# The output projection's weights in four column quarters, and two pieces of TensorE work moved, in a decoder step's attention

## The chip, the cores and the metric

The kernel runs on one core of a Trainium2 chip, in one launch. The metric is the device time of that core in microseconds, the median over several runs. The core's engines are TensorE (PE), VectorE (DVE), ScalarE (ACT) and GpSimd (POOL); SyncE (SP) issues most of the transfers. Each engine works through its own list of instructions in order, and waits on semaphores for the others.

## The reference

One layer of a decoder is computed for 512 prompt tokens and for 8 samples of one token each, with D = 1024 channels, all in f32. Each of its three sub-layers ends in `x <- LayerNorm(ALPHA * x + f(x))`:

1. a mixer (an RG-LRU group and a convolution group, side by side),
2. cross-attention with 4 heads of 256 into 256 memory tokens. Cut to what matters:

```
q = (x @ w_q)                     # 512 prompt tokens and 8 samples
s = q . k * 256**-0.5             # prompt: keys computed from mem_prompt; samples: keys from a cache
p = softmax(s)
o = p . v                         # samples: values from a cache
x = layer_norm(ALPHA * x + o @ w_o, ln2_g, ln2_b)
```

3. a mixture of experts: 64 routed experts, 8 per token, and a shared one.

The samples' cached keys and values are 8 times 256 x 1024 each (1 MB per sample), and `w_o` is 1024 x 1024 (4 MB).

## The kernel before

The engines' programs are written out by hand. Activations lie transposed, channels in 8 chunks of 128 partitions and the 520 tokens along the free dimension; the normalization behind the attention is done for two halves of 260 tokens, so that the first half is projected before the samples' values are summed. PSUM is used as four banks of 128 x 1024 (`bank`). The list `GROUPS` (L57 to L77) fixes which group of products takes which bank, in turn, and which engine empties it: `open_group` (L839) waits until the group four places earlier has been emptied, by ScalarE ("A") or VectorE ("V"). A group's place in this list is thus its place in TensorE's order.

The order of the attention is the list `ATTENTION` (L66), walked by TensorE (L1105) and by ScalarE (L1626): `sc0` to `sc3` are the prompt's scores for 128 tokens each, `pt0` to `pt3` the transposed probabilities, `o0` to `o7` the sums over the values for 128 channels each. Behind them come `xa0` to `xa7`, the output projection of the first half by chunks of 128 output channels (`project`, 8 products over the input channels each). Among these stand `ssT`, which turns the sampled scores, and `spT`, which turns their probabilities. Then follow `mean2a` (the mean over channels), `os` (the samples' sum over the cached values, 64 products for 8 samples) and inside it, ahead of the sixth sample, `var2a` (the variance). `osT` turns the result of `os` into the place of the 8 last tokens, and `xb0` to `xb7` project the second half.

VectorE computes the sampled scores itself (`sample_scores`, L2041): for each sample eight reductions of a product of cached keys and the query, copied to all partitions. At the end of sample b it raises `s_ss` to b + 1. Only then come the residuals of `xa0` and `xa1`, the softmax of the sampled scores (L2124 to L2128), the residuals of the further chunks, and `half_center`, `half_square_sum` and `half_scale` of the normalization. ScalarE squares (`half_squares`, L1646), takes the root of the variance (`half_root`, L1651), copies the four heads of `os` (L1670) and then `osT` (L1675), and applies gain and bias (`half_gain`).

Memory: `arena` has three parts of 8192 columns. During the sampled scores the first holds the queries of the 8 samples (`q_all`), the second the keys of samples 0 to 3 (`cache(1, b)`, 2048 columns each) and the third those of samples 4 to 7. `w_o` takes the whole second part as `wslot(1)`, in which each of the 8 rows of input channels has 1024 columns. The values take the places of the queries (samples 0 to 3) and of the keys in the third part (samples 4 to 7). SyncE (L521 to L532) therefore waits for `s_ss` at 2, loads value 0, waits for 4, loads `w_o` in four issues of 256 output columns each, then value 1, and so on; the five last values wait for all eight samples.

Of the kernel before, what the change touches and what calls it, by code (L numbers as in the profile page):

```python
# [14 lines left out]
P = 128  # L15
D = 1024
KC = D // P
# [32 lines left out]
for _n, _k in PAR_SPEC:  # L50
# [6 lines left out]
GROUPS = [(f"x{t}", "AV"[t % 2]) for t in range(TT)] + [("par", "V")]  # L57
# [6 lines left out]
GROUPS += [(f"q{c}", "A") for c in range(KC)] + [("qs", "A")]  # L64

ATTENTION = ["sc0", "sc1", "sc2", "pt0", "sc3", "pt1", "pt2", "pt3", "o0", "o1", "o2", "o3", "o4", "o5", "o6", "o7",  # L66
             "xa0", "xa1", "ssT", "xa2", "spT", "xa3"]
GROUPS += [(name, "V" if name[0] == "x" else "A") for name in ATTENTION]

GROUPS += [(f"xa{c}", "V") for c in range(4, KC)]  # L70
GROUPS += [("mean2a", "V"), ("var2a", "A"), ("os", "A"), ("osT", "A")]
GROUPS += [(f"xb{c}", "V") for c in range(KC)]
GROUPS += [("h1a0", "A"), ("mean2b", "V"), ("h3a0", "V"), ("var2b", "A"), ("h1b0", "A"), ("rt0", "A"),
           ("rt1", "A"), ("x20", "A"), ("rtT", "A"), ("x21", "A"), ("x22", "A")]
# [76 lines left out]
def decoder_step(nc: bass.Bass, ins, outs):  # L151
# [3 lines left out]
    with ExitStack() as ctx:  # L155
        def sb(name, shape, dt=F32):
            return ctx.enter_context(nc.sbuf_tensor(name, shape, dt))

        def sem(name):
            return ctx.enter_context(nc.semaphore(name))  # L160
# [5 lines left out]
        arena = sb("arena", [P, 3 * 8192])  # L166
# [19 lines left out]
        def rows(at, k):  # L186
            return act_mem[:, at:at + k * T].rearrange("p (k t) -> p k t", k=k)
# [34 lines left out]
        oT = rows(A3, KC)  # L222
# [4 lines left out]
        sp = mk_mem[0:32, 1344:1600]  # L227
# [82 lines left out]
        def value_cache(b):  # L310
            return cache(0, b) if b < 4 else cache(2, b - 4)

        def wslot(n):
            return arena[:, 8192 * n:8192 * n + 8192].rearrange("p (k n) -> p k n", k=KC)

        def cache(n, b):
            return arena[:, 8192 * n + 2048 * b:8192 * n + 2048 * b + 2048].rearrange("p (m n) -> p m n", m=2)

# [23 lines left out]
        s_wo_wd = [sem(f"s_wo_wd{n}") for n in range(4)]  # L342
# [37 lines left out]
        s_ss = sem("s_ss")  # L380
# [50 lines left out]
        def emptied(eng, g):  # L431

            who = GROUPS[g][1]
            n = sum(1 for _, w in GROUPS[:g + 1] if w == who)
            eng.wait_ge(s_emA if who == "A" else s_emV, n)

        def wait_out(eng, name):

            emptied(eng, GID[name])

        def wait_full(eng, name):
            eng.wait_ge(s_full, GID[name] + 1)

        def bank(name):
            return psum[:, PAIR.get(name, (GID[name] + 3) % 4), :]
# [15 lines left out]
        def _(sp):  # L461
# [12 lines left out]
            def big_cache(n, slot, src, b0):  # L474
                for b in range(4):
                    sp.dma_start(cache(slot, b), src[0, b0 + b].rearrange("(p m) h d -> p m (h d)", m=2)).then_inc(
                        s_load[n], 16)
# [38 lines left out]
            def values(b):  # L516
                sp.dma_start(value_cache(b), I["cache_mem_v"][0, b].rearrange("(p m) h d -> p m (h d)", m=2)).then_inc(
                    s_val[b // 2], 16)


            sp.wait_ge(s_ss, 2)  # L521
            values(0)
            sp.wait_ge(s_ss, 4)
            w_o = I["w_o"][0].rearrange("(k p) n -> p k n", p=P)
            for n in range(4):
                sp.dma_start(wslot(1)[:, :, 256 * n:256 * n + 256], w_o[:, :, 256 * n:256 * n + 256]).then_inc(s_wo_wd[n], 16)
            values(1)
            sp.wait_ge(s_ss, 6)
            values(2)
            sp.wait_ge(s_ss, NS)  # L530
# [307 lines left out]
        def _(pe):  # L838
            def open_group(name):  # L839
                g = GID[name]  # L840
                if g >= 4:
                    emptied(pe, g - 4)
                return bank(name)

            def mm(out, lhsT, rhs, first, last):
                return pe.matmul(out, lhsT, rhs, start=first, stop=last)  # L846
# [65 lines left out]
            for j in range(first, 2 * RC):  # L912
                if j == RC:
                    turn_states()
                name = ("zv", "zs")[j // RC] + str(j % RC)
                wide(name, lambda k: wslot(0)[:, k, j * P:(j + 1) * P], lambda k: xT[:, k, :], range(KC))
            pe.wait_ge(s_load[1], 16 * KC)
            for j in range(2 * RC):
                name = ("zu", "zg")[j // RC] + str(j % RC)
                at = (j + RC) % (2 * RC)  # L920
# [167 lines left out]
            def half_wide(name, w, act, ks, h, before=None):  # L1088

                ps = open_group(name)  # L1090
                for n, k in enumerate(ks):
                    if before is not None:
                        before(k)
                    last = mm(ps[:, 0:HALF], w(k), act(k)[:, HALF * h:HALF * h + HALF], n == 0, n == len(ks) - 1)
                last.then_inc(s_full, 1)

            def project(name, h):
                j = int(name[2])
                if h == 0 and j % 2 == 0:
                    pe.wait_ge(s_wo_wd[j // 2], 16)  # L1100
                if (h, j) == (0, 0):
                    wait_out(pe, "o7")
                half_wide(name, lambda k: wslot(1)[:, k, j * P:(j + 1) * P], lambda k: oT[:, k, :], range(KC), h)

            for name in ATTENTION:  # L1105
                if name == "ssT":
# [7 lines left out]
                else:  # L1114
                    {"sc": scores, "pt": turn_probs}[name[0:2]](int(name[2]))

            for c in range(4, KC):
                project(f"xa{c}", 0)

            def half_mean(name, h, turn_no):  # L1120
# [3 lines left out]
            def half_var(name, h):  # L1124
                pe.wait_ge(s_sqsum, h + 1)
                half_wide(name, lambda k: mean_d[:, :], lambda k: xsum[:, 0, :], range(1), h)
# [3 lines left out]
            wait_out(pe, "spT")  # L1130
            ps = open_group("os")
            for b in range(NS):
                if b == 5:
                    half_var("var2a", 0)
                if b % 2 == 0:
                    pe.wait_ge(s_val[b // 2], 16 * 2)
                for m in range(2):
                    for h in range(XH):
                        last = mm(ps[32 * h:32 * h + NS, 0:XD], weigh[:, m, h, b, :],
                                  value_cache(b)[:, m, XD * h:XD * h + XD], (b, m) == (0, 0), (b, m) == (NS - 1, 1))  # L1140
            last.then_inc(s_full, 1)
            wait_out(pe, "os")
            pe.wait_ge(s_os, XH - 1)
            ps = open_group("osT")
# [4 lines left out]
            for c in range(KC):  # L1149
                project(f"xb{c}", 1)  # L1150
# [163 lines left out]
            def down_few(b, part):  # L1314
                _, wd = ew(part)
                for k in range(2):
                    for h in range(2):
                        last = mm(psum[LCAP * h:LCAP * h + LCAP, 0, 0:512], hidT[:, b, LCAP * k:LCAP * k + LCAP],
                                  wd[:, k, 512 * h:512 * h + 512], k == 0, k == 1)
                return last  # L1320
# [11 lines left out]
            def down(b, part, cap=CAP):  # L1332
                _, wd = ew(part)
                for n in range(2):
                    for k in range(2):
                        last = mm(psum[0:cap, 0, 512 * n:512 * n + 512], hidT[:, b, cap * k:cap * k + cap],
                                  wd[:, k, 512 * n:512 * n + 512], k == 0, k == 1)
                return last
# [161 lines left out]
        def _(act):  # L1500
# [22 lines left out]
            for j in range(2 * RC):  # L1523
                c = j % RC
# [118 lines left out]
            def half(ap, h):  # L1643
                return ap[:, HALF * h:HALF * h + HALF]

            def half_squares(h):  # L1646
                for k in range(KC):
                    act.wait_ge(s_sub, norm_at[0] + k + 1)
                    act.activation(half(sq[:, k, :], h), half(xT[:, k, :], h), ACT.Square).then_inc(s_sq, 1)  # L1649

            def half_root(name, h):  # L1651
                wait_full(act, name)
                act.activation(half(rstd[:, :], h), bank(name)[:, 0:HALF], ACT.Sqrt, bias=eps_t[:, 0:1]).then_inc(s_emA, 1)
# [10 lines left out]
                act.activation(half(sh1[:, "ab".index(name[2]), :], h), bank(name)[:, 0:HALF], ACT.Silu).then_inc(s_emA, 1)  # L1664

            half_squares(0)
            half_root("var2a", 0)
            wait_full(act, "os")
            for h in range(XH):
                last = act.activation(o_s[:, XD * h:XD * h + XD], bank("os")[32 * h:32 * h + NS, 0:XD], ACT.Copy)  # L1670
                if h < XH - 1:
                    last.then_inc(s_os, 1)
            last.then_inc(s_emA, 1)
            wait_full(act, "osT")
            act.activation(oT[:, :, SEQ:T], bank("osT")[:, 0:64].rearrange("p (j b) -> p j b", j=KC), ACT.Copy).then_inc(s_emA, 1)  # L1675
            half_gain(0)
# [161 lines left out]
        def _(dve):  # L1838
# [202 lines left out]
            def sample_scores(b):  # L2041
                if b % 4 == 0:
                    dve.wait_ge(s_load[6 + b // 4], 16 * 4)
                if b % 2 == 0:
                    dve.wait_ge(s_qall[b // 2], 16 * 2)
                kc = cache(1 + b // 4, b % 4)
                for m in range(2):
                    for h in range(XH):
                        ins = dve.tensor_tensor_reduce(junk, kc[:, m, XD * h:XD * h + XD], q_all[:, b, XD * h:XD * h + XD],  # L2049
                                                       1.0, 0.0, ALU.mult, ALU.add, ss[:, m, 4 * b + h:4 * b + h + 1])  # L2050
                        if (m, h) != (1, XH - 1):
                            link(ins)
                ins.then_inc(s_ss, 1)
                dve.wait_ge(s_ss, b + 1)
# [443 lines left out]
```

## Time and profile before

| | |
|---|---|
| median of 3 runs | 1148.14 us |
| lowest and highest run | 1147.12 and 1151.25 us |
| span of the profiled execution (the page gives no other time of it) | 1144.5 us |
| PE busy | 1087.3 us, 95% |
| DVE, ACT, POOL busy | 43%, 25%, 21% |
| chain that ended last, by engine | PE 73%, DVE 17%, DMA 5%, ACT 2% |
| mean granted TensorE clock | 0.989 |

A row of a timeline gives the start in the span, the time it took, engine, line, operation, the tiles written and read, their shapes and the number of instructions merged; in square brackets stands how long the engine had been idle just before and who released it. A product of f32 operands appears as two records, so a chunk of 8 products has 16. A granted clock of 1.00 is 2.4 GHz and 0.50 is 1.2 GHz.

### The profile page before, as it was taken

The page shows a single profiled execution, that of the slowest core. Times are in us where ns is not written, and L with a number is a line of the kernel's source. Part 1 is how long each engine was busy: PE and PEld are TensorE (multiplying, and loading weights), DVE is VectorE, ACT ScalarE, POOL GpSimd, SP SyncE. Part 2 cuts the span into 40 slices and gives each one's busy share as a digit, 9 for nine tenths or more (in the row PEclk, how much of TensorE's full clock was granted, in tenths as well). Part 3 has the DMA queues.
Part 4 walks back from the last instruction along what each step waited for, and adds up shares of the span by engine and source line. Part 5 has one row for each costly group of instructions (what it writes and reads, how often), then busy time and mean ns, then how long its engine had stood idle before and what let it go on. Part 6 is the DMA issues. An engine that isn't in the chain of part 4 may idle for free.

```text
span 1144.5 us, 22216 instructions
## 1 busy us (share of the span) xinstructions
PE 1087.3 (95%) x8721; PEld 718.2 (63%) x8721; DVE 495.5 (43%) x1429; ACT 288.6 (25%) x615; POOL 243.9 (21%) x300
## 2 busy tenths in 40 slices
PE   7999998999997989989999999999999999999996
PEld 6888665877883857847555555555556555565531
DVE  0349999224028444681323333233343333423236
ACT  1112163004033041411223222222222322222220
POOL 3120040000000001031333323333333333343300
PEclk9999999999999999998999999999999999999998
DMA  9630315016034853175999999999999999999696
GB/s 331 271 147 1 147 32 183 2 60 251 3 119 148 323 200 133 56 288 217 394 404 409 412 411 415 408 410 414 410 417 410 403 421 407 409 416 387 256 387 262
DMA packets 67122, 319.77 MB, mean 279 GB/s; under 512 B 11069, under 2 KB 17429, under 8 KB 40397
## 3 DMA queue, kind: packets, MB, share of 16 engines
q1 hardware_dynamic: 51269, 278.60, 61.2%
q0 software_dynamic: 14336, 35.48, 8.2%
q10 hardware_dynamic: 1424, 4.35, 1.0%
q8 instruction: 70, 1.15, 0.4%
q14 instruction: 23, 0.19, 0.0%
HBM read 299.36 MB, written 28.58 MB: 287 GB/s over the span
## 4 chain that ended last, share of the span: by engine, by line
PE 73%; DVE 17%; DMA 5%; ACT 2%; issue 2%; SPq 0%; POOL 0%; DVEq 0%; ACTq 0%; POOLq 0%
PE psum L846 65%; PE psum L861 8%; DVE act_mem L1884 7%; DVE mk_mem L2049 2%; DMA arena<-y_rows 2%; DMA mk_mem<-x_rows,idx_x 2%; DMA arena<-in_w_in_dram 2%; DVE act_mem L2105 0%; ACT act_mem L1649 0%; DVE act_mem L2256 0%; DVE act_mem L1984 0%; ACT act_mem L1658 0%; DVE act_mem L2268 0%; DVE act_mem L1982 0%; DVE act_mem L1952 0%
## 5 line engine op out<-in xcount | busy, mean ns | idle before, releaser
L846 PE MATMUL psum<-arena,act_mem 128*32 128x128 f32 (+6 forms) x5488 | 493.4, 365 | 2.1 <-ACT act_mem L1764 1.1
L846 PEld LDWEIGHTS psum<-arena,act_mem 128*32 128x32 f32 (+4 forms) x5488 | 254.4, 120 | 192.6 <-issue 96.7
L846 PE MATMUL psum<-act_mem,arena 128*128 128x260 f32 (+1 forms) x1472 | 328.7, 386 | 8.9 <-DMA arena<-in_w_o_dram 3.8
L846 PEld LDWEIGHTS psum<-act_mem,arena 128*128 128x128 f32 x1472 | 281.0, 196 | 54.1 <-DMA arena<-in_w_o_dram 4.7
L861 PE MATMUL psum<-ident,act_mem 128*128 128x128 f32 (+6 forms) x488 | 79.3, 291 | 15.6 <-DMA act_mem<-in_x_prompt_dram 4.5
L754 POOL DMA_INDIRECT y_rows<-act_mem,idx_y x35 | 39.2, 1120 | 237.4 <-DVE act_mem L2319 214.4
L2317 DVE COPY act_mem<-psum 64x512 f32<-64x512 f32 x35 | 24.3, 693 | 124.7 <-PE psum L846 124.7
L1884 DVE SCALAR_TENSOR_TENSOR act_mem<-act_mem,wcb 128x511 f32<-128x511 f32 (+29 forms) x120 | 77.8, 730 | 0.1
L861 PEld LDWEIGHTS psum<-ident,act_mem 128*128 128x128 f32 (+6 forms) x488 | 57.3, 169 | 29.1 <-issue 17.5
L846 PEld LDWEIGHTS psum<-act_mem 128*96 128x96 bf16 (+5 forms) x419 | 29.9, 123 | 58.2 <-issue 54.6
L2310 DVE SCALAR_TENSOR_TENSOR act_mem<-act_mem,psum 128x128 f32<-128x128 f32 x35 | 12.2, 348 | 114.3 <-ACT act_mem L1720 114.3
L1716 ACT ACTIVATE act_mem<-psum 128x768 f32<-128x768 f32 (+1 forms) x63 | 45.1, 716 | 55.5 <-PE psum L861 55.5
L846 PE MATMUL psum<-act_mem 128*96 128x6 bf16 (+7 forms) x419 | 56.5, 262 | 2.0 <-ACT act_mem L1739 1.3
L1720 ACT ACTIVATE act_mem<-psum 128x192 f32<-128x192 f32 x35 | 11.6, 331 | 162.6 <-PE psum L846 162.6
L861 PE MATMUL psum<-ident,mk_mem 128*128 128x128 f32 (+4 forms) x316 | 43.7, 281 | 7.3 <-issue 4.0
L861 PEld LDWEIGHTS psum<-ident,mk_mem 128*128 128x128 f32 (+4 forms) x316 | 36.9, 183 | 19.2 <-issue 14.8
L747 POOL DMA_INDIRECT y_rows<-act_mem,idx_y x26 | 26.7, 1026 | 93.8 <-ACT act_mem L1755 52.9
L846 PE MATMUL psum<-arena,kv_mem 128*128 128x512 f32 x96 | 41.8, 593 | 1.2 <-ACT kv_mem L1539 1.2
L1745 ACT ACTIVATE act_mem<-psum 64x512 f32<-64x512 f32 x35 | 20.7, 591 | 77.1 <-PE psum L846 77.1
L680 POOL MEMSET act_mem<- 128x512 f32 x1 | 0.5, 525 | 184.2 <-PE psum L861 184.2
L754 POOL DMA_INDIRECT y_rows<-act_mem,more_y x35 | 34.6, 989 | 10.7 <-DVE idx_x L2286 5.8
L1506 ACT ACTIVATE act_mem<-psum,par 128x520 f32<-128x520 f32 x24 | 16.1, 696 | 77.0 <-PE psum L846 76.8
(291 smaller groups left out, 890.8 us busy)
## 6 DMA issues: line engine op xcount, KB each, us to landing
arena<-in_w_e_dram SPq DMA_DIRECT2D x192, 1024.0 KB, 10.2
arena<-y_rows SPq DMA_DIRECT2D x8, 2048.0 KB, 20.4
arena<-in_w_in_dram SPq DMA_DIRECT2D x16, 512.0 KB, 17.7
arena<-in_cache_mem_k_dram SPq DMA_DIRECT2D x8, 1024.0 KB, 8.6
arena<-in_cache_mem_v_dram SPq DMA_DIRECT2D x8, 1024.0 KB, 11.8
arena<-in_w_v_dram SPq DMA_DIRECT2D x1, 4096.0 KB, 24.4
arena<-in_w_k_dram SPq DMA_DIRECT2D x1, 4096.0 KB, 13.9
arena<-in_w_out_dram SPq DMA_DIRECT2D x1, 4096.0 KB, 14.1
```

Source lines behind the costliest of these rows:

```text
L747: gp.indirect_dma_start(out=y_rows[:, :].rearrange("r (h n) -> (r h) n", h=2), out_offset=bass.IndirectOffsetOnAxis(ap=idx_y[:, n:n + 1], ...
L754: gp.indirect_dma_start(out=y_rows[:, :], out_offset=bass.IndirectOffsetOnAxis(ap=idx[0:cap, n:n + 1], axis=0), in_=src[at:at + cap, :], i ...
L846: return pe.matmul(out, lhsT, rhs, start=first, stop=last)
L861: return pe.transpose(out, in_, ident[0:n, 0:n])
L1506: act.activation(out, two(bank(name)), func, **kw).then_inc(s_emA, 1)
L1716: return act.activation(xgT[:, b, :, 0:cap], psum[:, 1, :].rearrange("p (k s) -> p k s", k=KC)[:, :, ROWS_AT:ROWS_AT + cap], ACT.Copy)
L1720: return act.activation(silu[:, b, 0:192], psum[:, 2, 512 * b:512 * b + 192], ACT.Silu)
L1745: act.activation(out[0:LCAP, 0:512], psum[0:LCAP, 0, 0:512], ACT.Copy)
L1884: return dve.scalar_tensor_tensor(out, in0, w, in1, ALU.mult, ALU.add)
L2049: ins = dve.tensor_tensor_reduce(junk, kc[:, m, XD * h:XD * h + XD], q_all[:, b, XD * h:XD * h + XD], 1.0, 0.0, ALU.mult, ALU.add, ss[:, m ...
L2310: dve.scalar_tensor_tensor(silu[:, b, 0:P], silu[:, b, 0:P], gates[:, n, 0:1], psum[:, 2, 512 * b + 192:512 * b + 320], ALU.mult, ALU.mult)
L2317: dve.tensor_copy(out[0:LCAP, 512:1024], psum[LCAP:2 * LCAP, 0, 0:512])
```

## The change

`w_o` still comes in four issues of 256 output columns, but each lies in one piece of 2048 columns, `out_quarter(n)`, which is exactly the place of the keys of sample n. SyncE issues quarter n when `s_ss` has reached n + 1, and values 0 and 1 behind the second and the fourth quarter. `ssT` stands behind `xa3` and `spT` behind `xa4`. On TensorE `var2a` stands behind the whole of `os`; on ScalarE the root of `var2a` stands behind the four copies of `os` and ahead of the copy of `osT`; the group list follows. VectorE's program is not edited.

```
 ATTENTION = [..., "o7",
-             "xa0", "xa1", "ssT", "xa2", "spT", "xa3"]
+             "xa0", "xa1", "xa2", "xa3", "ssT", "xa4", "spT"]
-GROUPS += [(f"xa{c}", "V") for c in range(4, KC)]
-GROUPS += [("mean2a", "V"), ("var2a", "A"), ("os", "A"), ("osT", "A")]
+GROUPS += [(f"xa{c}", "V") for c in range(5, KC)]
+GROUPS += [("mean2a", "V"), ("os", "A"), ("var2a", "A"), ("osT", "A")]
...
+        def out_quarter(n):
+            return arena[:, 8192 + 2048 * n:8192 + 2048 * n + 2048].rearrange("p (k n) -> p k n", k=KC)
...
-            sp.wait_ge(s_ss, 2)
-            values(0)
-            sp.wait_ge(s_ss, 4)
             w_o = I["w_o"][0].rearrange("(k p) n -> p k n", p=P)
             for n in range(4):
-                sp.dma_start(wslot(1)[:, :, 256 * n:256 * n + 256], w_o[:, :, 256 * n:256 * n + 256]).then_inc(s_wo_wd[n], 16)
-            values(1)
+                sp.wait_ge(s_ss, n + 1)
+                sp.dma_start(out_quarter(n), w_o[:, :, 256 * n:256 * n + 256]).then_inc(s_wo_wd[n], 16)
+                if n % 2 == 1:
+                    values(n // 2)
             sp.wait_ge(s_ss, 6)
             values(2)
...
-                half_wide(name, lambda k: wslot(1)[:, k, j * P:(j + 1) * P], lambda k: oT[:, k, :], range(KC), h)
+                at = P * (j % 2)
+                half_wide(name, lambda k: out_quarter(j // 2)[:, k, at:at + P], lambda k: oT[:, k, :], range(KC), h)
...
-            for c in range(4, KC):
+            for c in range(5, KC):
                 project(f"xa{c}", 0)
...
             for b in range(NS):
-                if b == 5:
-                    half_var("var2a", 0)
                 if b % 2 == 0:
                     pe.wait_ge(s_val[b // 2], 16 * 2)
...
             last.then_inc(s_full, 1)
+            half_var("var2a", 0)
             wait_out(pe, "os")
...
             half_squares(0)
-            half_root("var2a", 0)
             wait_full(act, "os")
             for h in range(XH):
                 last = act.activation(o_s[:, XD * h:XD * h + XD], bank("os")[32 * h:32 * h + NS, 0:XD], ACT.Copy)
...
             last.then_inc(s_emA, 1)
+            half_root("var2a", 0)
             wait_full(act, "osT")
```

## Rows read from the trace of the kernel before

**Rows 1.** Waits between 345 and 460 us: who waited, for whom, total, times, longest.
```profile
PE psum L846 <- DMA arena<-in_w_o_dram: 3.8, 1, 3.8
```

**Rows 2.** Timeline of TensorE in the attention stretch.
```profile
351.52 13.97 PE L846 MATMUL psum<-act_mem,kv_mem 128*128 128x512 f32 x32 [1.20 <-ACT act_mem L1620]
369.33 8.97 PE L846 MATMUL psum<-act_mem,arena 128*128 128x260 f32 x32 [3.84 <-DMA arena<-in_w_o_dram]
379.07 0.38 PE L861 MATMUL psum<-ident,mk_mem 128*32 128x128 f32 x2 [0.77 <-DVE mk_mem L2049]
...
383.18 17.80 PE L846 MATMUL psum<-act_mem,arena 128*128 128x260 f32 x80
402.03 0.70 PE L846 MATMUL psum<-act_mem,mean_d 128*128 128x260 f32 x2 [1.05 <-DVE act_mem L2079]
402.67 4.50 PE L846 MATMUL psum<-arena,act_mem 128*8 128x256 f32 x80
...
409.60 2.78 PE L846 MATMUL psum<-arena,act_mem 128*8 128x256 f32 x48
414.07 0.66 PE L861 MATMUL psum<-ident,mk_mem 8*128 8x8 f32 x8 [1.70 <-ACT mk_mem L1670]
415.04 33.51 PE L846 MATMUL psum<-act_mem,arena 128*128 128x260 f32 x144 [0.31 <-ACT act_mem L1675]
```

**Rows 3.** Stretches: length, busy time of each engine, granted clock, DMA share, GB/s.
```profile
351.50:365.50 14.00, 13.97 (x32) 5.99 (x32) 12.96 (x61) 4.18 (x7) 0.00 (x0) 1.00 0.23 79
...
369.30:375.00 5.70, 5.67 (x18) 4.66 (x19) 5.28 (x25) 0.00 (x0) 0.00 (x0) 0.70 1.10 349
393.00:401.00 8.00, 7.98 (x37) 6.58 (x35) 1.71 (x4) 0.00 (x0) 0.00 (x0) 1.00 0.21 89
415.00:420.00 5.00, 4.96 (x15) 4.06 (x16) 0.00 (x0) 4.98 (x9) 1.18 (x5) 0.66 1.11 360
```

**Rows 4.** Timeline of VectorE: sampled scores (first and last of 128 instructions), centring, sum of squares.
```profile
349.08 0.42 DVE L2049 CUSTOM_DVE_ANT_0 mk_mem<-arena 128x256 f32<-128x256 f32 x1
...
378.84 0.08 DVE L2049 DVE_READ_ACCUMULATOR2_ANT mk_mem<- 128x1 f32 x1
...
402.78 2.77 DVE L2089 TENSOR_TENSOR act_mem<-act_mem,psum 128x260 f32<-128x260 f32 x8 [0.80 <-PE psum L846]
...
406.16 2.75 DVE L2105 TENSOR_TENSOR act_mem<-act_mem 128x260 f32<-128x260 f32 x6
```

**Rows 5.** Issues on SyncE's queue: start, time in the queue, line.
```profile
364.00 5.42 SPq L526 DMA_DIRECT2D arena<-in_w_o_dram  x4
369.46 11.71 SPq L517 DMA_DIRECT2D arena<-in_cache_mem_v_dram  x7
```

**Rows 6.** The source view of L526, the four issues of w_o.
```profile
DMA to landing us min/median/max: 5.3/9.5/12.6
```

**Rows 7.** Timeline of ScalarE: three table loads and what stands around them.
```profile
261.47 0.60 ACT L1594 ACTIVATE kv_mem<-psum 128x512 f32<-128x512 f32 x1 [1.20 <-PE psum L846]
262.09 1.28 ACT L1506 ACT_TABLE_LOAD   x1
...
365.53 0.60 ACT L1624 ACTIVATE act_mem<-psum 128x512 f32<-128x512 f32 x1 [1.12 <-PE psum L846]
...
406.08 1.28 ACT L1653 ACT_TABLE_LOAD   x1
409.71 0.48 ACT L1653 ACTIVATE rstd<-psum,eps_t 128x260 f32<-128x260 f32 x1 [2.35 <-PE psum L846]
412.44 1.58 ACT L1670 ACTIVATE mk_mem<-psum 8x256 f32<-8x256 f32 x4 [2.26 <-PE psum L846]
414.76 0.22 ACT L1675 ACTIVATE act_mem<-psum 128x64 f32<-128x64 f32 x1 [0.75 <-PE psum L861]
...
462.82 1.28 ACT L1664 ACT_TABLE_LOAD   x1
464.12 0.39 ACT L1664 ACTIVATE act_mem<-psum 128x260 f32<-128x260 f32 x1
```

## The prediction

> **What bounds the kernel now.** I read the waits of the attention stretch first, then TensorE's timeline there, then the granted clock of the same stretch, and then VectorE, SyncE's queue and ScalarE, each for the thing TensorE waits for. TensorE carries the end: the page has it busy for 95% of the span, and 73% of the chain that ended last is its own. So a microsecond is won only where TensorE stands still or runs slowly, and the change touches two such places. The waits name the first, 3.8 us for a transfer of `w_o` [rows 1]; the second is the cut in `os`, seen in the timeline.
>
> There the first place runs so: the values' product for the prompt (`o0` to `o7`) ends at 351.52 + 13.97 = 365.49, and the projection `xa0` starts at 369.33, after 3.84 us of waiting for `w_o` [rows 2]. Its two chunks `xa0`, `xa1` take 8.97 us, where five chunks (80 records) take 17.80, so 7.1 for two [rows 2]. The clock view says why: 1.00 before, 0.70 on average over 369.3 to 375.0 [rows 3], a stretch at the lower of the two levels (1.2 against 2.4 GHz). Lost there: 0.30 x 5.7 = 1.7 us. Then 0.77 us of waiting for the sampled scores ahead of `ssT` [rows 2]. The second place: `os` runs its first five samples in 4.50 us, `var2a` blocks the queue, the last three samples run at 409.60, then ScalarE's copies, `osT`, a copy, and `xb0` starts at 415.04; the clock is down again there, 0.66 over 415 to 420, so 0.34 x 5 = 1.7 us [rows 2, 3].
>
> **Part 1: `w_o` by quarters.** VectorE's sampled scores run from 349.08 to 378.84 + 0.08 = 378.92, 3.73 us a sample, so samples 0 to 3 end at 352.8, 356.5, 360.3 and 364.0 [rows 4]. Before, all four issues stand behind the fourth of these, at 364.00 [rows 5]. After, quarter n goes when sample n is done. The number and size of the transfers stay: four of 1 MB. Landing took 5.3 to 12.6 us, the upper figure with five other megabytes in the queue [rows 6]. Even by the slowest, the quarters are there at 365.4, 369.1, 372.9 and 376.6, while their first readers start no sooner than 366.2 (`xa0`), 373.2 (`xa2`), 380.6 (`xa4`) and 388 (`xa6`). The wait for `w_o` goes away.
>
> What is late next is ScalarE's copy of `o7`, which frees the operand: 365.53 + 0.60 = 366.13 [rows 7]. So `xa0` starts at about 366.18: gain 369.33 - 366.18 = 3.15 us. A gap of 0.7 us remains there. The clock was 1.00 throughout `o0` to `o7` behind a gap of 1.20 [rows 2, 3], so I take it to stay up: gain 1.7 us, with 0 as the other end.
>
> On SyncE's queue the moved issues pass values(0) and values(1). values(0) now goes behind two quarters and values(1) still behind the fourth; neither is read before `os`, 30 us later. values(3) to (7) keep their release, the last sampled score, and were issued by 369.46 + 11.71 = 381.17 [rows 5]. Their queue is emptier, since three megabytes of `w_o` have left earlier: no loss, and a gain only where somebody waits for them, which nobody does. Do the earlier writes slow VectorE while it reads keys? Samples 0 to 3 took 364.00 - 349.08 = 14.92 us with hardly a transfer running (DMA share 0.23), samples 4 to 7, beside transfers at full rate (1.10), 378.92 - 364.00 = 14.92 as well [rows 3 to 5]: nothing is charged.
>
> **Part 2: `ssT` two chunks later.** `xa0` to `xa3` take at most 4 x 3.56 = 14.2 us from 366.18 and end near 380.4, behind the last sampled score at 378.92. The wait of 0.77 us goes: gain 0.77 (a bank wait cannot replace it: `ssT` takes `xa0`'s bank, which VectorE frees 0.5 us behind its last score). VectorE's order does not change: `xa0`, `xa1`, then the maximum of `ssT`, now at about 380.8 instead of 380.3. The 0.5 us does not reach TensorE, because `xa4` (3.5 us) lies between `ssT` and `spT`, as `xa2` did before. If that cover were gone, it would cost those 0.5 us.
>
> So the projections end at 383.18 + 17.80 = 400.98 before, and 3.15 + 1.70 + 0.77 = 5.62 us sooner after: 395.36. The mean's wait and product keep their length, and `os` starts at 402.67 - 5.62 = 397.05.
>
> **Part 3: `var2a` behind `os`.** `os` took 409.60 + 2.78 - 402.67 = 9.71 us with `var2a` and its wait inside; its two pieces alone are 4.50 + 2.78 = 7.28. Gain 2.43: `os` ends at 404.33. The wait added to PE's queue is for the square sum. VectorE's chain from the mean to that sum took 402.78 to 406.16 + 2.75 = 408.91 [rows 4]; 5.62 sooner that is 403.29, 1.0 us ahead of the end of `os`. So `var2a` does not wait and lies beside ScalarE's copies of `os` (4 in 1.58 us).
>
> What this part costs lies on ScalarE. The copies of `os` now come ahead of the square root, whose function table must be loaded, 1.28 us. A load stands right in front of the instruction that needs it, also behind a waiting copy: at L1594 the copy waits until 261.47, and the load follows it at 262.09 although ScalarE was idle before [rows 7]. So load and root now lie between the copies and the copy of `osT`: 0.02 + 1.28 + 0.02 + 0.48 + 0.02 + 0.22 + 0.06 = 2.10 us from the last copy's end to `xb0`, where it was 415.04 - 414.02 = 1.02. `osT` itself (0.66) is covered by the load. Loss 1.08. The ends: if the load were hidden in the wait ahead of the copies, as it was in the wait ahead of the root until now, nothing of its 1.28 would remain and the loss would be zero (`osT` then ends last); 1.08 is the other end, and I take it.
>
> The Trainium skill, "ScalarE: Activation LUTs", section "What ACT_TABLE_LOAD costs", speaks against the move: it counts about 2.66 us for each switch, a drain of 1.38 beside the load. The trace has a switch with nothing to wait for, and there the next instruction started 464.12 - 462.82 = 1.30 us after the load began, right behind the work ahead of it [rows 7]. By the page the time would be an estimated 1.4 us longer, 1142.5; the trace does not bear it out, and it has its place below as (e).
>
> **Sum.** 5.62 + 2.43 - 1.08 = 6.97 us sooner at the start of `xb0` (408.07 instead of 415.04). The remaining term is the clock at `xb0`. Before, it fell behind a gap of 1.70 and a short burst [rows 2, 3]. After, TensorE runs through `os` and `var2a` without a stop to 405.0, then has gaps of about 1.0 and 1.4 us around `osT`. Behind the 1.05 at `mean2a` it stayed up (the records of `os` take 56 ns each there, 58 in the second piece), behind 1.70 it fell, and the new gaps lie between these or near the lower one; bounds 0 and a gain of 1.7 us. I take 0, since the burst between the gaps is again only `osT`.
>
> Behind `xb0` everything is released in turn: `w1_s` and expert 0 by the end of `os`, expert 1 by `xb7`, the further experts by the routing that follows. All of it shifts with TensorE; `half_scale` on VectorE ends near 412.5, and the first residual `xb0` is full no sooner than 411.6, with three more banks free. So the profiled execution's 1144.5 us becomes 1137.5. The page gives no time of that execution but its span; the median of the runs, 1148.14, is 3.64 above, and I leave that as it is: 1137.5 + 3.6 = 1141.1 us.
>
> **Rivals.** (a) The clock stays up at `xb0` too: another 1.7 us, 1139.4. For it: the gaps are each shorter than the one that preceded the fall. Against: together they are longer. Chance 0.27.
> (b) The gain is partly given back by TensorE's clock, which falls once or twice more in places where the shifted work leaves short bursts, at 1.7 us each: 1142.8 to 1144.5. Chance 0.10. For it: two falls in 50 us already, neither needing more than a few microseconds of gaps.
> (c) The later stages do not follow: the expert loop starts at its old time, and the gain is hidden, 1148. For it: the DMA engines are busy for over 90% of the expert loop. Against: what starts their stream waits for TensorE or for the routing. That the quarters arrive no sooner than before, so that the edit does not do what it says, belongs here too, and the landing times speak against it. Chance 0.06.
> (d) Slower. `var2a`, and with it the normalization, stands behind all eight values, where it needed six before. Place: the last pair inside `os`, needed at about 397.05 + 0.75 x 7.28 = 402.5. Every microsecond that it lands later delays `xb0` by one; it eats the whole gain from 409.5 on, and a landing at 415.5 gives 1154. Against: the DMA engines were at 0.21 over 393 to 401 [rows 3], so the last value was down at about 395, and now it has less ahead of it. Chance 0.03.
> (e) The switch to the root's table costs more than its load, because ScalarE must first finish the copies. The most that the rows allow from a load's start to its root is 409.71 - 406.08 = 3.63 us, which holds a wait for TensorE [rows 7]; that is 2.3 us over the 1.30 taken, 1143.4. Against: the row of 1.30. Chance 0.04. (The table rule of the Trainium skill quoted above is of this kind.)
>
> **How the numbers follow.** The forecast has the remaining 0.50. About 0.5% (5.7 us) is what a measurement of this kernel can tell from no change; the border lies at 1142.4. The forecast lies 1.3 us below it, and the runs shown spread over 4 us, so 0.43 of its 0.50 counts as faster, with 0.26 of (a) and 0.05 of (b) and (e): 0.74. Slower: (d), 0.03. The rest, 0.23, is no change. The range reaches from (a) with 2 us for the runs' spread and a clock fall less later on, 1137.4, to the end of (b), 1144.7.
>
> **What would show it.** In the changed kernel's timeline the gap behind `o7` should be about 0.7 us and released by ScalarE's copy; `xa0` to `xa3` should take 14 us at a clock of 1.00; `ssT` should follow without a wait; `os` should be one piece of 7.3 us; ScalarE should show copies, table load, root, copy in that order; and `xb0` should start near 408. The prediction is wrong if `xa0` still waits for a transfer, if `os` waits for a value, if the load is found ahead of the copies, or if `xb0` starts 7 us sooner and the span does not follow.

## The result and the profile after

The changed kernel took 1141.34 us in the median (1139.96 to 1143.96) beside 1147.63 before (four runs now, where the table ahead of the prediction has three): a ratio of 0.9936, with a 95% interval of 0.9916 to 0.9956, or 7.3 us less. The two medians differ by 6.3 us; here and below, what is called less or more in us is worked out from the ratio and the median before. Measured again beside some of the experiments (`e7_changed_again` below) it was 0.9949 (0.9929 to 0.9969), 5.9 us less. The forecast was 1141.1, 7 us less.

Of TensorE's timeline these rows answer to [rows 2]. Line numbers are 3 higher after the change: L846 is now L849, L861 is L864.

```profile
349.67 1.22 PE L864 MATMUL psum<-ident,act_mem 128*128 128x128 f32 x8 [2.00 <-DVE act_mem L2039]
351.67 1.97 PE L864 MATMUL psum<-ident,act_mem 128*128 128x128 f32 x8 [0.78 <-DVE act_mem L2039]
354.84 16.90 PE L849 MATMUL psum<-act_mem,kv_mem 128*128 128x512 f32 x32 [1.21 <-ACT act_mem L1623]
372.47 14.27 PE L849 MATMUL psum<-act_mem,arena 128*128 128x260 f32 x64 [0.73 <-issue]
386.58 0.38 PE L864 MATMUL psum<-ident,mk_mem 128*32 128x128 f32 x2
...
402.48 0.71 PE L849 MATMUL psum<-act_mem,mean_d 128*128 128x260 f32 x2 [1.05 <-DVE act_mem L2082]
403.11 7.09 PE L849 MATMUL psum<-arena,act_mem 128*8 128x256 f32 x128
410.13 0.70 PE L849 MATMUL psum<-act_mem,mean_d 128*128 128x260 f32 x2
411.90 0.66 PE L864 MATMUL psum<-ident,mk_mem 8*128 8x8 f32 x8 [1.06 <-ACT mk_mem L1672]
413.81 31.83 PE L849 MATMUL psum<-act_mem,arena 128*128 128x260 f32 x144 [1.25 <-ACT act_mem L1678]
```

The reader is to see three things. `xa0` starts 0.73 us behind `o7` instead of 3.84 (the row names no releaser, but ScalarE's copy of `o7` ends at 371.78 + 0.60 = 372.38, just ahead of it), and `xa0` to `xa3` are one piece of 14.27 us. `ssT` follows without any wait. `os` is one piece of 7.09 us. And one thing that was not forecast: `o0` to `o7` took 16.90 us where they had taken 13.97. The stretches (columns as in [rows 3]) say why: the clock was down behind the softmax's gaps here, and up at `xb0`, the reverse of before. A stretch in which the granted clock goes down to the lower of its two levels is called a fall below.

```profile
349.60:354.80 5.20, 3.19 (x16) 2.42 (x16) 4.28 (x21) 3.48 (x7) 0.52 (x1) 0.59 0.00 0
354.80:371.80 17.00, 16.90 (x32) 7.09 (x32) 15.75 (x73) 4.20 (x8) 0.00 (x0) 0.83 0.92 312
372.40:386.60 14.20, 14.13 (x65) 12.20 (x66) 9.60 (x43) 0.00 (x0) 0.00 (x0) 1.00 0.63 236
...
413.80:419.00 5.20, 5.20 (x24) 4.53 (x25) 4.79 (x10) 3.05 (x7) 0.28 (x1) 1.00 1.09 313
```

ScalarE, answering to [rows 7]: copies of `os`, table load, root, copy of `osT`. The root follows its load after 1.29 us.

```profile
410.27 1.57 ACT L1672 ACTIVATE mk_mem<-psum 8x256 f32<-8x256 f32 x4 [3.77 <-PE psum L849]
411.87 1.28 ACT L1656 ACT_TABLE_LOAD   x1
413.16 0.48 ACT L1656 ACTIVATE rstd<-psum,eps_t 128x260 f32<-128x260 f32 x1
413.54 0.22 ACT L1678 ACTIVATE act_mem<-psum 128x64 f32<-128x64 f32 x1
```

SyncE's queue, answering to [rows 5], and the landing of `w_o`, answering to [rows 6]: the quarters go two by two between the values, and the slowest lands in 7.0 us instead of 12.6.

```profile
355.25 4.12 SPq L528 DMA_DIRECT2D arena<-in_w_o_dram  x2
359.41 0.58 SPq L521 DMA_DIRECT2D arena<-in_cache_mem_v_dram  x1
362.72 4.11 SPq L528 DMA_DIRECT2D arena<-in_w_o_dram  x2
366.87 17.03 SPq L521 DMA_DIRECT2D arena<-in_cache_mem_v_dram  x7
...
DMA to landing us min/median/max: 5.1/5.7/7.0
```

The view that says most is one that the prediction does not use: the chain of waits of this stretch alone (345 to 420 us), its shares by line. Before:

```profile
by line: PE psum L846 40.7%; DVE mk_mem L2049 36.1%; issue 5.0%; DVE act_mem L2105 3.5%; ACT act_mem L1649 3.3%; ACT act_mem L1610 2.6%; ACT mk_mem L1670 2.0%; PE psum L861 1.7%; DVE small L2023 1.6%; DVE act_mem L2036 1.2%; DVE act_mem L20
```

and after:

```profile
by line: PE psum L849 82.0%; PE psum L864 3.3%; ACT act_mem L1613 2.6%; issue 2.1%; ACT mk_mem L1672 2.0%; ACT L1656 1.7%; DVE small L2026 1.6%; ACT act_mem L1623 1.4%; DVE act_mem L2039 1.2%; ACT rstd L1656 0.6%; DVE act_mem L2082 0.6%; DV
```

VectorE's sampled scores (L2049) carried 36% of this stretch before, from the softmax up to `ssT`; after the change they are gone from the chain, and TensorE's products carry 82%. The wait for `w_o` was thus not a wait that set the end by itself: it lay beside the scores.

### The profile page after: what moved, and what is told of

The parts are those of the page before. It is cut to its first block, busy times and chain, and to the rows that moved or that the text cites. A ratio compares the mean times of both kernels' runs of the same rounds, so it can differ in the third digit from the quotient of the medians.

```text
span 1142.2 us, 22216 instructions
## 1 busy us (share of the span) xinstructions
PE 1090.5 (95%) x8721; PEld 719.4 (63%) x8721; DVE 495.1 (43%) x1429; ACT 288.6 (25%) x615; POOL 243.5 (21%) x300
## 4 chain that ended last, share of the span: by engine, by line
PE 80%; DVE 14%; DMA 2%; ACT 2%; issue 2%; SPq 0%; POOL 0%; DVEq 0%; ACTq 0%; POOLq 0%
PE psum L849 72%; PE psum L864 8%; DVE act_mem L1887 7%; DMA arena<-in_w_in_dram 2%; DMA mk_mem<-x_rows,idx_x 1%; DVE act_mem L2259 0%; DVE act_mem L1987 0%; ACT act_mem L1661 0%; DVE act_mem L2271 0%; DVE act_mem L2108 0%; DVE act_mem L1985 0%; DVE act_mem L1955 0%; DVE act_mem L1959 0%; DVE act_mem L1956 0%; DVE act_mem L1957 0%
## 5 line engine op out<-in xcount | busy, mean ns | idle before, releaser
L849 PE MATMUL psum<-arena,act_mem 128*32 128x128 f32 (+6 forms) x5488 | 494.6, 366 | 2.1 <-ACT act_mem L1767 1.1
L849 PEld LDWEIGHTS psum<-arena,act_mem 128*32 128x32 f32 (+4 forms) x5488 | 254.7, 121 | 192.9 <-issue 96.7
L849 PE MATMUL psum<-act_mem,arena 128*128 128x260 f32 (+1 forms) x1472 | 326.7, 385 | 7.4 <-DMA arena<-in_w_in_dram 3.2
L849 PEld LDWEIGHTS psum<-act_mem,arena 128*128 128x128 f32 x1472 | 280.1, 195 | 51.6 <-issue 4.0
L864 PE MATMUL psum<-ident,act_mem 128*128 128x128 f32 (+6 forms) x488 | 80.5, 293 | 17.4 <-issue 4.3
L864 PEld LDWEIGHTS psum<-ident,act_mem 128*128 128x128 f32 (+6 forms) x488 | 57.9, 170 | 31.5 <-issue 18.0
L849 PEld LDWEIGHTS psum<-act_mem 128*96 128x96 bf16 (+5 forms) x419 | 29.9, 123 | 59.0 <-issue 55.4
L849 PE MATMUL psum<-act_mem 128*96 128x6 bf16 (+7 forms) x419 | 56.5, 262 | 2.0 <-ACT act_mem L1742 1.3
L864 PE MATMUL psum<-ident,mk_mem 128*128 128x128 f32 (+4 forms) x316 | 43.7, 281 | 4.1 <-issue 3.1
L864 PEld LDWEIGHTS psum<-ident,mk_mem 128*128 128x128 f32 (+4 forms) x316 | 37.0, 183 | 15.6 <-issue 13.4
L849 PE MATMUL psum<-arena,kv_mem 128*128 128x512 f32 x96 | 41.8, 593 | 1.2 <-ACT kv_mem L1542 1.2
```

The source lines that it names most:

```text
L864: return pe.transpose(out, in_, ident[0:n, 0:n])
```

## The experiments

All are compared with the kernel before on the same chip, in 6 to 12 timed runs each. In the traces I use one length that does not depend on when the kernel's start was over: from the last turn of probabilities (`pt3`) to the start of `os`. It was 402.67 - 349.22 = 53.45 us before and 403.11 - 351.67 = 51.44 in the changed kernel's trace above. The two last turns of before, `pt2` and `pt3`:

```profile
347.22 1.09 PE L861 MATMUL psum<-ident,act_mem 128*128 128x128 f32 x8 [2.01 <-DVE act_mem L2036]
349.22 1.09 PE L861 MATMUL psum<-ident,act_mem 128*128 128x128 f32 x8 [0.91 <-DVE act_mem L2036]
```

**The change without its third part** (`e1_no_var_move`): the changed kernel with these lines put back, and on ScalarE the root ahead of the copies again.

```
-GROUPS += [("mean2a", "V"), ("os", "A"), ("var2a", "A"), ("osT", "A")]
+GROUPS += [("mean2a", "V"), ("var2a", "A"), ("os", "A"), ("osT", "A")]
...
+                if b == 5:
+                    half_var("var2a", 0)
```

> The quarters and the later ssT, with var2a inside os and its root ahead of the copies as in the kernel before. Theory (the sum of the prediction): the first two parts bring 3.15 + 1.70 + 0.77 = 5.6 us by themselves, the third 1.35 more; so about 1142.0 us beside 1147.6 before, xa0 starting 0.7 us behind o7, and 9.7 us again for os with var2a inside. Rival: the gain of the change is mostly the clock falling less often by chance; then this kernel stands where the changed one does, 1141.3, or back at 1147.6, without regard to the part left out.

Measured: 0.9971 (0.9954 to 0.9988), 3.3 us less (1.4 to 5.3), short of the 5.6. In its trace `pt3` to `os` took 47.63 us, 5.82 less than before, as the sum had it; here the clock stayed up in the whole stretch. That falls there in the other executions make up the difference fits the two traces of the changed kernel, but is not shown run by run.

```profile
350.56 1.09 PE L864 MATMUL psum<-ident,act_mem 128*128 128x128 f32 x8 [0.90 <-DVE act_mem L2040]
352.86 13.97 PE L849 MATMUL psum<-act_mem,kv_mem 128*128 128x512 f32 x32 [1.21 <-ACT act_mem L1624]
367.56 14.27 PE L849 MATMUL psum<-act_mem,arena 128*128 128x260 f32 x64 [0.73 <-issue]
...
398.19 4.50 PE L849 MATMUL psum<-arena,act_mem 128*8 128x256 f32 x80
...
409.59 0.66 PE L864 MATMUL psum<-ident,mk_mem 8*128 8x8 f32 x8 [1.69 <-ACT mk_mem L1674]
410.56 31.83 PE L849 MATMUL psum<-act_mem,arena 128*128 128x260 f32 x144 [0.31 <-ACT act_mem L1679]
```

The last two rows also show that at `xb0`, behind the very gaps of [rows 2] (1.7 and 0.31), the clock did not fall this time: 31.83 us for the piece that took 33.51 before. The same gaps bring the clock down in one execution and not in another.

**The third part alone** (`e2_var_move_alone`): the kernel before with the last hunks of the diff only.

```
+GROUPS += [("mean2a", "V"), ("os", "A"), ("var2a", "A"), ("osT", "A")]
...
             last.then_inc(s_full, 1)
+            half_var("var2a", 0)
```

> Only the third part on top of the kernel before: os in one piece, var2a behind it, its root behind the copies. Theory: os 2.4 us shorter, 1.1 us given back by the table load and the root ahead of the copy of osT; xb0 1.35 us sooner against the end of xa7, so about 1146.3 us. Rival: the table load is no loss (it was hidden or would be anyway): 1145.2; or the wait for the square sum is only moved: 1147.6.

Measured: 0.9974 (0.9960 to 0.9989), 3.0 us less; the lower end of the interval is 1.3. In the trace `os` starts at 403.79 and `xb0` at 414.48: 10.69 us where it was 12.37, a gain of 1.68, somewhat above the 1.35. What the timing shows beyond that is not explained.

```profile
403.79 7.09 PE L846 MATMUL psum<-arena,act_mem 128*8 128x256 f32 x128
...
414.48 31.83 PE L846 MATMUL psum<-act_mem,arena 128*128 128x260 f32 x144 [1.25 <-ACT act_mem L1674]
```

**The quarters alone** (`e3_quarters_alone`): the first part without the later `ssT` and without the third part.

```
-             "xa0", "xa1", "xa2", "xa3", "ssT", "xa4", "spT"]
+             "xa0", "xa1", "ssT", "xa2", "spT", "xa3"]
```

> Only the quarters: w_o by quarters as each sample's scores end, ssT and spT in their old places, var2a inside os. Theory: xa0 starts 3.15 us sooner and runs at the upper clock, xa1 ends 5 us sooner, and all of it is lost again in front of ssT, whose wait for the last sampled score grows from 0.8 to about 5.6 us; xa2 starts where it did, and the time is the one before, 1147.6 (a clock fall behind the longer wait may add to it or take the place of the one that went). Rival: the parts add up independently, and this one alone brings 4.85 us: 1142.8.

Measured: 1.0023 (1.0008 to 1.0038), 2.6 us more. The edit that takes the 3.84 us of waiting away makes the kernel slower when it is alone.

```profile
350.28 1.97 PE L864 MATMUL psum<-ident,act_mem 128*128 128x128 f32 x8 [0.50 <-DVE act_mem L2040]
353.45 13.97 PE L849 MATMUL psum<-act_mem,kv_mem 128*128 128x512 f32 x32 [1.21 <-ACT act_mem L1624]
368.16 7.25 PE L849 MATMUL psum<-act_mem,arena 128*128 128x260 f32 x32 [0.73 <-issue]
380.15 0.58 PE L864 MATMUL psum<-ident,mk_mem 128*32 128x128 f32 x2 [4.74 <-DVE mk_mem L2053]
380.52 4.88 PE L849 MATMUL psum<-act_mem,arena 128*128 128x260 f32 x16
```

`xa0` and `xa1` run early and at the upper clock, then TensorE waits 4.74 us for the sampled scores; `ssT` comes 29.87 us after `pt3`, before it was 29.85. Nothing is won, and the clock now falls behind this longer wait, in `xa2`, where it is on the path (4.88 us for 3.67). `pt3` to `os` took 54.78 us, 1.33 more than before, which lies in the interval of 0.9 to 4.4; the chain of waits of this stretch has VectorE's scores at 36.2%, as before.

**The table loaded early** (`e4_table_early`): the changed kernel with one line more.

```
             half_squares(0)
+            act.activation(small[:, 42:43], eps_t[:, 0:1], ACT.Sqrt)
             wait_full(act, "os")
```

> The changed kernel with one more instruction on ScalarE: a root of one column ahead of the wait for os, so that the table is loaded while ScalarE waits. Theory: the copies of os are followed by the root at once; os to xb0 takes 2.6 to 2.7 us instead of 3.6, and the time is 1.0 us less than the changed kernel's, about 1140.3. Rival: the load is not what the copy of osT waits for (osT or the root is): no change, 1141.3.

Measured: 0.9935 (0.9908 to 0.9962), 7.5 us less than before. Beside the changed kernel's 7.3 and 5.9 the timing does not resolve the microsecond; the trace does:

```profile
404.05 1.28 ACT L1670 ACT_TABLE_LOAD   x1
405.34 0.20 ACT L1670 ACTIVATE small<-eps_t 128x1 f32<-128x1 f32 x1
407.80 1.57 ACT L1673 ACTIVATE mk_mem<-psum 8x256 f32<-8x256 f32 x4 [2.26 <-PE psum L849]
409.40 0.48 ACT L1656 ACTIVATE rstd<-psum,eps_t 128x260 f32<-128x260 f32 x1
410.12 0.22 ACT L1679 ACTIVATE act_mem<-psum 128x64 f32<-128x64 f32 x1 [0.24 <-PE psum L864]
```

The load lies in ScalarE's wait for `os`, the root follows the copies at once, and `os` (400.64) to `xb0` (410.40) took 9.76 us instead of 10.70: 0.94 of the 1.08 that the prediction charged to the load.

**TensorE delayed ahead of `o0`, in the kernel before and in the changed one** (`e5_before_late_o0`, `e6_changed_late_o0`), and the changed kernel again beside them. The same edit in both:

```
                 if j == 0:
+                    for _ in range(5):
+                        mm(ps[:, 0:SEQ], mean_d[:, :], v_tok[:, 0, 0:SEQ], True, True)
                     wait_out(pe, "pt3")
```

> The kernel before with five further products of 128x512 on TensorE ahead of o0, whose results are overwritten; they fill 1.2 us of waiting and push o0 to o7 back by about 3.15 us. New theory: before the change the stretch from pt3 to ssT is carried by VectorE's sampled scores (29.85 us in the before and in the quarters-alone traces alike), and TensorE had 3.15 us of slack at o7 and 0.77 more ahead of ssT; so the time stays that of the kernel before. Rival (TensorE carried this stretch already, as the prediction's sum by TensorE's own waits suggests when its terms are taken singly): 3.15 us longer.

> The changed kernel with the same five further products ahead of o0. New theory: the change moves this stretch from VectorE to TensorE, so that what delays o0 to o7 (a clock fall at the softmax's gaps among it) is now paid in full: 3.15 us longer than the changed kernel. Rival: the stretch has slack as before, no change against the changed kernel.

> The changed kernel again, beside the others on one chip. The prediction's sum gives 7 us less than before; the parts alone measured 3.7 and 3.0 us, together 6.7. With the new theory the gain is the 7 us less what TensorE's clock falls cost in o0 to o7 now that they are not hidden (about 1 us on average over runs): 6 us. Rival: the parts help each other beyond their sum: 8 us or more.

Measured against before: the delayed kernel before 0.9995 (0.9980 to 1.0010), no change; the delayed changed kernel 0.9988 (0.9974 to 1.0001), and the changed one 0.9949 (0.9929 to 0.9969). So the same delay costs nothing before (0.6 us less, within the interval) and 4.5 us after, where 3.15 was expected, with an uncertainty of some 2.8. The traces say the same more closely: from `pt2` to `os` it took 55.45 us before and 55.39 with the delay, 51.90 in the changed kernel of the same runs and 55.28 with the delay, 3.38 more. In the delayed kernel before, the clock had also fallen at `pt2` and `pt3` (0.57 over 347.5 to 351.5), and this too was hidden: it still waited 2.06 us ahead of `ssT`.

```profile
347.87 3.79 PE L861 MATMUL psum<-ident,act_mem 128*128 128x128 f32 x16 [2.01 <-DVE act_mem L2038]
...
379.72 0.38 PE L861 MATMUL psum<-ident,mk_mem 128*32 128x128 f32 x2 [2.06 <-DVE mk_mem L2051]
...
403.26 4.50 PE L846 MATMUL psum<-arena,act_mem 128*8 128x256 f32 x80
```

The changed kernel's second trace (`e7_changed_again`) shows the exposed fall again, `o0` to `o7` in 15.36 us and 49.90 from `pt3` to `os`, and at `xb0` the clock was down there (33.49 us for the piece).

```profile
351.89 1.97 PE L864 MATMUL psum<-ident,act_mem 128*128 128x128 f32 x8 [0.91 <-DVE act_mem L2039]
355.07 15.36 PE L849 MATMUL psum<-act_mem,kv_mem 128*128 128x512 f32 x32 [1.20 <-ACT act_mem L1623]
```

**TensorE kept at work in its waits** (`e8_filled`, `e10_filled_more`, `e11_before_filled`). The first adds products of 128x128, whose results are overwritten, to the kernel with the early table load; the second has eight more ahead of `rtT`; the third has the first's products in the kernel before.

```
+            def fill(name, n):
+                ps = open_group(name)
+                for _ in range(n):
+                    mm(ps[:, 0:P], mean_d[:, :], ident[:, :], True, True)
...
+                    fill(f"pt{t}", 6 if t == 2 else 2)
...
+                    fill("o0", 3)
...
+            fill("osT", 3)
...
+            fill("var2b", 9)
```

Twelve such products stand ahead of `hlast` too. Of the names, `hlast` turns the mixer's last states, `qs` the samples' queries, `h1a0` is the shared expert's chunk behind `xb7`, `var2b` the variance of the second half, and `rtT` turns the router's scores.

> The changed kernel with the early table load (1.0 us) and with TensorE kept at work by short products, whose results are overwritten, in its waits ahead of hlast, pt2, pt3, o0, osT and var2b. Theory (the waits bring the clock down, about 1.7 us a time, at hlast and var2b in nearly every trace, at pt2 to o0 in some): the falls at hlast and var2b go, 3.4 us, and those at o0 to o7, about 1 us on average; together with the table 5 to 6 us less than the changed kernel. Rival: the clock falls from time to time whatever TensorE does, or the products delay what waits behind them: 1 us less than the changed kernel, or none.

> The kernel before with the short products alone, at the same six places, without the change and without the early table. Theory: the falls at hlast and var2b go (3.4 us); what falls at pt2 to o0 was hidden behind VectorE's scores here, so keeping the clock up there brings nothing, and the fall at xa0 behind the wait for w_o stays and is hidden as well: 3.4 us less than before, and up to 1.7 more where the fall at xb0 goes too. Rival (the change and the products are worth the same everywhere): as from the changed to the filled kernel less 1.0 for the table, 4.5 us or more; or the clock does not follow the waits here: no change.

> The filled kernel with eight more short products ahead of rtT, where in its trace the clock fell behind a gap of 2.69 us. Theory: that fall goes too, 1.7 us less than the filled kernel; about 12 to 13 us less than before. Rival: the fall is followed by waits for ScalarE and VectorE (the routing), which hide it: no change, 11 us less than before.

Measured: the filled kernel 0.9901 (0.9874 to 0.9929), 11.4 us less than before and 5.5 less than the changed kernel of the same runs, with an uncertainty of some 4. The kernel with the early table alone stood 7.5 below before, on another chip; the 3.9 from there to the filled kernel, the products' own share, has an uncertainty of some 4.4. In the filled kernel's trace `pt3` to `os` takes 47.58 us and `xb0` to `h1a0` 31.83, the lengths without a fall. The products alone, in the kernel before: 1.0012 (0.9994 to 1.0031), no gain. The expectation of 3.4 us failed, and its trace tells where:

```profile
368.55 8.97 PE L846 MATMUL psum<-act_mem,arena 128*128 128x260 f32 x32 [3.62 <-DMA arena<-in_w_o_dram]
378.57 0.38 PE L861 MATMUL psum<-ident,mk_mem 128*32 128x128 f32 x2 [1.06 <-DVE mk_mem L2061]
...
452.96 0.71 PE L846 MATMUL psum<-act_mem,mean_d 128*128 128x260 f32 x2 [0.71 <-DVE act_mem L2117]
...
464.77 0.72 PE L861 MATMUL psum<-ident,kv_mem 64*128 64x64 f32 x5 [2.69 <-ACT kv_mem L1698]
465.43 3.35 PE L861 MATMUL psum<-ident,act_mem 128*128 128x128 f32 x16
```

The stretch up to `ssT` has VectorE's length again (29.84 us). At `var2b` the fall is gone, but the products behind it only end sooner and wait 2.69 us ahead of `rtT`, and the clock falls there (3.35 us for 1.97). From `xb0` to ScalarE's copy of the first gathered rows (at 512.31) it took 97.8 us with this fall, 97.9 before (with the falls at `xb0` and `var2b`), and 96.2 in the changed kernel, whose trace has the fall at `var2b` only: so that one was hidden, and the one at `rtT` is not. The trace of `e1` shows the same without any added product: no fall at `var2b`, 2.69 us of waiting ahead of `rtT`, a fall there, and 97.8 us. What the products won at `hlast` (1.2 us up to `qs`) is below what these runs resolve.

With the eight products at `rtT`: 0.9902 (0.9882 to 0.9922), 11.3 us less than before, 1138.2 us. The trace shows 96.2 us behind `xb0`, 1.7 less than the filled kernel; the timing shows no difference between the two, so that this step is left as seen in one trace only. Its rows are the stretch without a fall:

```profile
348.32 1.09 PE L864 MATMUL psum<-ident,act_mem 128*128 128x128 f32 x8 [0.45 <-DVE act_mem L2053]
349.25 0.83 PE L849 MATMUL psum<-ident,mean_d 128*128 128x128 f32 x6
350.52 14.00 PE L849 MATMUL psum<-act_mem,kv_mem 128*128 128x512 f32 x32 [0.44 <-ACT act_mem L1636]
365.26 14.27 PE L849 MATMUL psum<-act_mem,arena 128*128 128x260 f32 x64 [0.73 <-issue]
```

**The second part alone** (`e9_scores_later_alone`): the kernel before with only the new `ATTENTION` list.

```
-             "xa0", "xa1", "ssT", "xa2", "spT", "xa3"]
+             "xa0", "xa1", "xa2", "xa3", "ssT", "xa4", "spT"]
```

> Only the second part: ssT behind xa3 and spT behind xa4, w_o as before in one place and var2a inside os. Theory (VectorE carried the stretch, and each of the first two parts needs the other): xa0 still starts behind the transfer, and xa0 to xa3 run on with the clock fall that follows that wait; ssT no longer waits: 0.8 us less than before where the clock falls, 2.5 where it does not. Quarters alone measured 2.6 us more, quarters and this together 3.3 to 3.7 less; so this alone should be 1 to 2 us less than before, not the 6 that plain addition of the two measurements would give it. Rival (plain addition): 6 us less.

Measured: 0.9999 (0.9983 to 1.0015), no change; 1 us of gain lies inside the interval, 6 does not. Its trace is another case than the one expected: the clock fell at `pt3` and was down for a part of `o0` to `o7` (17.00 us for 13.97), which thus ended so late that `w_o` was there and `ssT` had nothing to wait for; `pt3` to `os` took 51.54 us, 1.91 less than before. The timing shows no such gain over twelve runs.

```profile
357.51 17.00 PE L846 MATMUL psum<-act_mem,kv_mem 128*128 128x512 f32 x32 [1.20 <-ACT act_mem L1620]
```

So plain addition is out: neither of the two parts gains alone (2.6 more, 0), and together they give 3.3.

## Why the prediction was right, point by point

- *The wait for `w_o` goes and 0.7 us remain.* Right: 0.73 us, and all quarters landed in 7.0 us or less (7.8 in the slowest of the traces that have them). VectorE's scores took 29.85 us from first to last beside the earlier transfers, as before.
- *`xa0` to `xa3` at the upper clock.* Right in every trace that has the quarters (14.27 us, or 7.25 for two).
- *`ssT` without a wait.* Right.
- *The sum of the three, 5.62 us up to `os`.* Right in size: 5.82 in the trace without a clock fall. Its three terms were taken for independent gains, and this was wrong: 3.15 and 1.70 lay beside VectorE's scores. The experiment with the quarters alone gave neither, and the delayed kernel before shows that 3 us of TensorE's time there cost nothing. "With 0 as the other end" for the clock at `xa0` was no end at all, because that fall was hidden. What the change really does is move two chunks, `xa2` and `xa3` (7.1 us), from behind VectorE's scores to beside them, for which the quarters make room. The gain is less than 7.1 because TensorE is now the later of the two: in the trace of `e1` the scores end at 380.28 and `ssT` starts at 381.66.
- *`os` 2.43 us shorter, 1.08 given back on ScalarE.* Right: 12.37 us from `os` to `xb0` became 10.70, 1.67 net against 1.35. The load did follow the copies and cost what its row said: the root started 1.29 us after the load did, so the longer switch of rival (e) is out. The drain of 1.38 us that the Trainium skill counts for a switch ("ScalarE: Activation LUTs", "What ACT_TABLE_LOAD costs") is not in this trace; the table moved early gave 0.94 us back.
- *The clock at `xb0`, bounds 0 and 1.7.* It stayed up in the first trace of the changed kernel, as in rival (a), and fell in the second; both ends occur, as they do with the old order.
- *Missed: the fall at `pt2` to `o7`.* The prediction took the clock of that place from one trace, and its loss is now paid: 2.9 us of products in the first trace, 1.4 in the second. Rival (b), a gain partly given back by clock falls, comes nearest; but it placed them at short bursts that the shifted work leaves, and this fall stands ahead of them, at gaps that both kernels have.
- *`xb0` near 408, the span 1137.5.* Not so in the profiled execution: 413.81 and 1142.2. Of the 5.74 us, 2.45 had passed by `pt3` already, and the fall took 3.81 (0.88 in `pt3`, 2.93 in `o0` to `o7`); the two gains beat the sum by 0.20 and 0.32. From `pt3` to `xb0` this trace is 3.68 us shorter than before, not 6.97.
- *7 us in all.* Right in the median, and in part by luck. Timed singly, the first two parts gave 3.3 us (5.3 at most) where the sum has 5.62, and the third gave 3.0 (1.3 at least) where it has 1.35; the two differences offset each other. Rivals (c) and (d) are out: behind `xb0` the first trace of the changed kernel takes 728.4 us to the end of the span, 729.5 before, and `os` waited for no value.
- *Span to median, 3.64 us.* The runs of the changed kernel list a time 1.8 us above their own span (1143.96 and 1142.2), so about 1.9 of the 3.64 were the luck of the profiled execution of before. It was left as a constant, and did no harm because only the difference of the two kernels was worked out.

## What to carry to other kernels

A wait on the busiest engine is worth its length only if that engine carries the chain there: read the chain of the stretch, not of the whole span, before waits are added up. Two waits that go back to the same producer, here VectorE's scores, can be one wait: taking away the first only lengthened the second, from 0.77 to 4.74 us. When an edit makes the stretch pass to another engine, look again at what used to be hidden on that engine; here it was clock falls, and short throwaway products in TensorE's gaps, worth nothing that the timing shows before the change, went with a kernel 5.5 us faster after it (the early table load among it; the products' own share is not resolved).

## What the runs showed of the hardware that was not expected

The granted clock's falls differ from one execution to the next for the same program and the same gaps. Behind gaps of 2.0, 0.8 to 0.9 and 1.2 us (`pt2`, `pt3`, `o0`) it fell in both traces of the changed kernel and stayed up in those of `e1` and `e4`, whose program is the same up to there; at `xb0` behind 1.7 and 0.31 us it fell before and stayed up in `e1`. Of the ten traces without filled gaps, six have it down somewhere in `pt2` to `o7`, and six at `xb0`. With the gaps filled, 0.8 us and less being left, it fell at none of these places in three traces, which are few. The runs agree as far as the mean granted clock goes: 0.993 to 0.995 in the last filled kernel and 0.988 to 0.994 in the first, where the kernel before had 0.979 to 0.991. That filled gaps make the times steadier is not shown: 6 runs of the last filled kernel lie between 1136.1 and 1138.9 us, but 6 of the first between 1134.4 and 1144.1, 12 of the products alone between 1144.8 and 1155.6, and 12 of `e1` between 1142.5 and 1149.6.
